# A one-core hybrid encoder layer: 896 columns of the expert table streamed and 1152 gathered, with a re-ordered ScalarE queue and filler matmuls

## What is computed

```python
scores = einsum('thcd,hcnd->thcn', q, keys)        # 8 heads, two halves of 128 keys
s_top, i_top = top_k(scores, 16)                   # 16 best of each half
best, pos = top_k(all 16*16 sums, 16)              # 16 experts for each head
idx = i*128 + j                                    # 128 experts for each token
gate = softmax(best)
hid = gelu(einsum('td,thkd->thk', x, U[idx]))      # U is 16384 x 2048
out = einsum('thk,thkd->td', gate * hid, V[idx])   # V is 16384 x 2048
```

## Time and profile before

| | us |
|---|---|
| median of 3 runs (2125.72 to 2132.07) | 2126.39 |
| the profiled execution: its own time | 2125.02 |
| its span, first to last instruction | 2123.0 |
| PE busy over the span | 2019.5 (95%) |
| DVE, ACT, POOL busy | 1508.4, 815.0, 835.2 |
| moved by DMA | 558.12 MB, mean 263 GB/s |
| mean granted TensorE clock | 0.911 |

### The profile page before, as it was taken

How to read it: one execution, slowest core, us unless ns; L and a number is a source line. 1 busy time by engine, 2 the same in 40 slices (tenths; PEclk the granted TensorE clock), 3 DMA queues, 4 the chain that set the end, 5 groups by cost and what they waited for, 6 DMA issues and landing times.

```text
span 2123.0 us, 27862 instructions
## 1 busy us (share of the span) xinstructions
PE 2019.5 (95%) x10247; PEld 1707.7 (80%) x10247; DVE 1508.4 (71%) x1987; ACT 815.0 (38%) x956; POOL 835.2 (39%) x626
## 2 busy tenths in 40 slices
PE   7999999999999999999999979997889999999997
PEld 6988998777888889988888757765556888888886
DVE  5465774556655557688888746666635999999998
ACT  4354433444434443222221223335436444444444
POOL 1001320000000001266654565566621888888782
PEclk9999999999999999999999965555559999999999
DMA  6555443445555565699999977677732999999996
GB/s 203 188 182 182 147 151 129 159 159 165 187 183 179 199 218 195 238 409 409 408 394 364 367 272 247 220 252 253 275 119 89 379 395 395 390 406 395 394 381 239
DMA packets 176353, 558.12 MB, mean 263 GB/s; under 512 B 19152, under 2 KB 22240, under 8 KB 175200
## 3 DMA queue, kind: packets, MB, share of 16 engines
q1 hardware_dynamic: 117744, 288.47, 38.6%
q0 software_dynamic: 58480, 267.94, 33.6%
HBM read 551.62 MB, written 4.72 MB: 262 GB/s over the span
## 4 chain that ended last, share of the span: by engine, by line
PE 77%; DMA 9%; DVE 6%; issue 3%; ACT 2%; POOL 2%; SPq 0%; DVEq 0%; POOLq 0%; ACTq 0%
PE acc L1918 7%; PE acc L1920 7%; PE acc L1919 7%; PE scr L2222 6%; PE acc L2180 5%; PE scr L2180 5%; PE acc L1901 4%; PE acc L1903 4%; PE acc L1904 4%; PE scr L2252 3%; DMA v_raw<-in_v_dense 3%; DMA ub<-in_u_dense 3%; PE acc L2306 3%; PE scr L2307 3%; PE acc L2307 3%
## 5 line engine op out<-in xcount | busy, mean ns | idle before, releaser
L1104 DVE TENSOR_TENSOR w_lo<-raw,w_hi 128x2048 fp32r<-128x2048 f32 x136 | 314.6, 2314 | 279.2 <-ACT w_hi L751 278.1
L751 ACT ACTIVATE w_hi<-raw 128x2048 fp32r<-128x2048 f32 x136 | 260.1, 1913 | 405.0 <-PE acc L1920 273.5
L707 POOL DMA_INDIRECT starts<-in_v_gather,expert x256 | 366.3, 1431 | 100.1 <-DVE X L1823 76.1
L684 POOL DMA_INDIRECT slots<-in_u_gather,expert x256 | 245.4, 959 | 269.2 <-DVE slots L1623 77.3
L1623 DVE SCALAR_TENSOR_TENSOR slots<-slots,acc 128x1280 f32<-128x1280 f32 x192 | 281.8, 1483 | 79.8 <-DMA slots<-in_u_gather,expert 78.2
L1042 ACT ACTIVATE v_hi<-v_raw 128x1344 fp32r<-128x1344 f32 x128 | 170.5, 1332 | 259.5 <-PE scr L2308 197.5
L1823 DVE SCALAR_TENSOR_TENSOR X<-starts,weight,X 128x704 f32<-128x704 f32 x256 | 242.1, 946 | 0.8 <-DMA starts<-in_v_gather,expert 0.4
L1918 PE MATMUL acc<-w_hi,hT_hi 128*128 128x512 f32 x576 | 227.6, 395 | 2.5 <-DVE w_lo L1104 2.5
L1919 PE MATMUL acc<-w_lo,hT_hi 128*128 128x512 f32 x576 | 225.3, 391 | 0.0
L1920 PE MATMUL acc<-w_hi,hT_lo 128*128 128x512 f32 x576 | 225.2, 391 | 0.0
L1840 DVE TENSOR_TENSOR v_lo<-v_raw,v_hi 128x1344 fp32r<-128x1344 f32 x128 | 199.3, 1557 | 8.8 <-issue 6.7
(11 more groups left out here) (322 smaller groups left out, 4003.6 us busy)
## 6 DMA issues: line engine op xcount, KB each, us to landing
raw<-in_w_in SPq DMA_DIRECT2D x88, 1024.0 KB, 5.1
v_raw<-in_v_dense SPq DMA_DIRECT2D x128, 672.0 KB, 7.5
ub<-in_u_dense SPq DMA_DIRECT2D x128, 384.0 KB, 7.2
raw<-in_w_o SPq DMA_DIRECT2D x16, 1024.0 KB, 5.1
raw<-in_peer_wq SPq DMA_DIRECT2D x16, 1024.0 KB, 5.3
raw<-in_w_a_up SPq DMA_DIRECT2D x8, 1024.0 KB, 5.0
raw<-in_w_b_up SPq DMA_DIRECT2D x8, 1024.0 KB, 5.1
slots<-in_u_gather,expert POOLq DMA_INDIRECT x256, 7.0
```

The source lines that it names most:

```text
L684: pool.indirect_dma_start(slots[j][:, :], None, u_gather[:, :], bass.IndirectOffsetOnAxis(ap=expert[:, t, k:k + 1], axis=0)).then_inc(row_ ...
L707: pool.indirect_dma_start(starts[j][:, :], None, v_gather[:, :], bass.IndirectOffsetOnAxis(ap=expert[:, s // NSEL, s % NSEL:s % NSEL + 1], ...
L751: a.activation(w_hi[:, m % 2, :, :], raw[:, m % 2, :, :], ACT.Copy).then_inc(hi_ready, 1)
L1104: v.tensor_tensor(w_lo[:, m % 2, :, :], raw[:, m % 2, :, :], w_hi[:, m % 2, :, :].bitcast(fp32), ALU.subtract).then_inc(lo_ready, 1)
```

## The change

Of U's 2048 columns seven blocks (896) are streamed and 1152 gathered. Streaming is spread over 162 gathers (40 groups) instead of 128 (32 groups), with three stream buffers of 3.5 KB for each partition instead of four of 3 KB. There are 21 row buffers of 4.5 KB instead of 20 of 5 KB; from gather 176 up to nine of them are open at a time, before it seven from gather 146 on (before: five to eight from gather 124 on, seven from 144). POOL multiplies a second row in every other group up to q = 112. In ScalarE's turn the evictions come first (`pairs`), and it sums the products of the group before; of a group's `hot_j` two stand ahead of that sum. The 64 picks are spread over 13 groups (41 to 53), the 32 first scatters over ten (54 to 63). Each pick has a filler matmul of 256 columns ahead of it; each first scatter has three of 512; and 16 of 512 stand behind the last dense block, ahead of the wait for the last eviction. The reads of kept rows have two buffers of the wider kind instead of three. The two halves of the residual have a semaphore each, the value gathers start five ahead instead of four, and the second streamed block of V is loaded with the first.

```diff
-UC = 6
+UC = 7
-UB_AT = (112, 120, 101, 104)
+UB_AT = (112, 120, 101)
+STREAMED = 162
+FOUR_GROUPS = STREAMED // FOUR
-CEN_GROUP = (13, 28)
-SELECT_FROM, SELECT_END = 34, 50
-MERGE_AT = 43
-GATE_TURN = 47
+CEN_GROUP = (15, 31)
+SELECTED_BY = 31
+SELECT_FROM, SELECT_END = 41, 54
+MERGE_AT = 48
+GATE_TURN = 51
-WARM_PICK, WARM_FIRST, WARM_LAST = 0, 0, 0
+WARM_PICK, WARM_FIRST, WARM_LAST, WARM_WAIT = 2 * P, 4 * P, 0, 16
+TWICE = 112
 def on_pool(q):
-    return q % FOUR == FOUR - 1 and FOUR <= q < GATHERS - 1 and q not in DVE_ALONE
+    return FOUR <= q < GATHERS - 1 and (q % FOUR == FOUR - 1 or q % (2 * FOUR) == 1 and q < TWICE)
+def pairs(i):
+    return [u for u in range(BLOCKS // 2) if 8 * u * FOUR_GROUPS // (4 * BLOCKS) == i]
 def parts(i):
-    return range(min(56, 2 * i), min(56, 2 * i + 2))
+    return range(min(56, 56 * i // SELECTED_BY), min(56, 56 * (i + 1) // SELECTED_BY))
...
                 for q in range(FOUR * n, FOUR * n + FOUR):
                     gather(q)
-                if on_pool(FOUR * n - 1):
-                    product(FOUR * n - 1)
+                for q in range(max(0, FOUR * n - FOUR), FOUR * n):
+                    if on_pool(q):
+                        product(q)
...
             for i in range(GROUPS):
+                for u in pairs(i):
+                    evict(u)
...
-                if 0 < i <= GROUPS // 2:
-                    evict(2 * i - 2)
-                    evict(2 * i - 1)
-                for b in selected(i):
+                sums = [q for q in range(max(0, FOUR * i - FOUR), FOUR * i) if on_pool(q)]
+                for b in selected(i)[0:2]:
+                    hot_j(b)
+                for q in sums:
+                    sum_product(q)
+                for b in selected(i)[2:]:
                     hot_j(b)
                 if i == SPREAD_FROM:
                     hot_first(0)
                 for n in spread(i):
                     hot_first(n + 1)
                     scatter_out(n)
-                if on_pool(FOUR * i + FOUR - 1):
-                    sum_product(FOUR * i + FOUR - 1)
...
+            pe.wait_ge(scr_free[1], use_number("score3"))
+            for n in range(WARM_WAIT):
+                warm(picked[0], GW)
             pe.wait_ge(evicted, BLOCKS // 2)
-            pe.wait_ge(scr_free[1], use_number("score3"))
             squares_j(0)
```

More of the change, by code:

```diff
@@ L135, in overwritten @@
         return None
-    return (P - 1 - (2 * block_at(j) + 9)) // 2
+    return int(P - 1 - (2 * (block_at(j) + ROW_KB) - 1)) // 2
 def row_open(j, q):
     if j < HELD_ROW:
-        return q < 2 * overwritten(j) - 4 and (q >= FOUR or j in FIRST_ROWS)
+        return q < 2 * overwritten(j) * STREAMED // P - 4 and (q >= FOUR or j in FIRST_ROWS)
     if j == HELD_ROW:
-        return FOUR <= q < P
-    return q >= (60 if j in SCORE_ROWS else 112 if j in ALL_ROWS else 144)
+        return FOUR <= q < 188
+    return q >= (64 if j in SCORE_ROWS else 128 if j in ALL_ROWS else 144 if j == NORM_ROW else 176)
 def row_table():
@@ L179, in selected @@
         return range(0)
-    per = NT * BATCHES // (SELECT_END - SELECT_FROM)
-    return range(per * (i - SELECT_FROM), per * (i - SELECT_FROM + 1))
+    n = SELECT_END - SELECT_FROM
+    return range(NT * BATCHES * (i - SELECT_FROM) // n, NT * BATCHES * (i - SELECT_FROM + 1) // n)
+def pairs(i):
+    return [u for u in range(BLOCKS // 2) if 8 * u * FOUR_GROUPS // (4 * BLOCKS) == i]
 def spread(i):
@@ L564, in _ @@
                 load_u(m)
[L565 to L568, removed]
+                for t in range(NT):
+                    if m == (FOUR * CEN_GROUP[t] + 6) * P // STREAMED:
+                        keep_rows(t)
             sp.wait_ge(cen_stored, 16 * NT)
+            sp.wait_ge(ones_ready, 1)
+            sp.sem_inc(granted_w, 1)
             for h in range(CHUNKS):
-                if h < 2:
-                    sp.wait_ge(ones_ready, h + 1)
-                    sp.sem_inc(granted_w, 1)
                 load_rows(h)
@@ L681, in gather @@
                     pool.wait_ge(u_used, BLOCKS)
-                    wait_rows(pool, HELD_ROW)
+                if first_use(q) and j == NORM_ROW:
+                    pool.wait_ge(product_ready, sum(map(on_pool, range(NSEL))))
                 pool.sem_inc(granted, 1)
@@ L1688, in centre, with ones @@
                                 ).then_inc(cen_ready, 1)
-            def ones(first):
+            def ones():
                 dve.wait_ge(cen_stored, 16 * NT)
-                if not first:
-                    dve.wait_ge(u_used, BLOCKS)
-                for room in (rows_a[0], rows_a[1], rows_b[0]) if first else (rows_a[2], rows_b[1], rows_b[2]):
+                for room in (*rows_a, *rows_b):
                     last = v.memset(room[:, :], 1.0)
@@ L1772, in _ @@
                             later_part(n)
-                    for b in selected(i)[q % FOUR:q % FOUR + 1]:
+                    n, at0 = len(selected(i)), q % FOUR
+                    for b in selected(i)[n * at0 // FOUR:n * (at0 + 1) // FOUR]:
                         find(b)
@@ L1782, in _ @@
                 if i == CEN_GROUP[1] + 3:
-                    ones(True)
-                if i == SELECT_FROM - 1:
-                    ones(False)
+                    ones()
                 if i in GATE_AT:
@@ L1795, in _ @@
                     copy_gate(0)
+                if i == SPREAD_FROM:
+                    wait_rows(dve, HELD_ROW)
                 for n in spread(i):
@@ L1806, in _ @@
             scatter_out(NT * BATCHES - 1)
-            dve.wait_ge(x_back, 16 * NT)
+            for t in range(NT):
+                dve.wait_ge(x_back[t], 16)
             def low_e(pair, t):
```

53 lines of the change are left out of this document (26 added, 27 removed).

## The result

The changed kernel takes 2322.0 us against 2128.7 before: the ratio is 1.091, with a 95% interval of 1.0885 to 1.0937. Slower was forecast, at 2200 us with a range up to 2235; the loss is 193 us where 75 were forecast. The profiled execution has a span of 2319.7 us.

What follows compares the result with a forecast made beforehand. Bounds: TensorE with DMA close by in the dense part, TensorE at half clock in picks, VectorE in values. Second scatters move from 1568 to 1643, +75 on 2125: 2200 us; case range 2180 to 2230, 8 in 10 from 2050 to 2235.

Steps and rivals of the forecast that it cites:

- Dense part, +55 for longer blocks: Dense part: fourteen TensorE instructions a block instead of twelve move its last matmul from 1230.4 to 1286 us, +55.
- the 17.6 us of waits: Dense part: TensorE's waits in the kernel before, 349.4 − 331.8, kept unchanged on top of 387 us of blocks.
- Three stream buffers: I take nothing: Dense part: three buffers need loads landing within about 5.6 us; nothing added to the sum, +46 us left to the range.
- a rival with a chance of 0.08: Dense part: the three-buffer ring binds, +46 us on the sum, 2246 us in all; chance 0.08.
- The argument that a shorter queue would bring the landing from 7.2 to 5.4 us: Dense part: a load has up to two others queued ahead instead of three, so the 7.2 us median becomes some 5.4.
- `keep_rows`, priced with other things at 0 to 10 us: Blocks 52 and 102, SP's queue: late rows stall the ring at most 10 us; with ScalarE's evictions, 0 to +10 together.
- The gap and the clock: Between dense part and picks: first pick after 11 us, some 7 us of TensorE idle, picks at clock 0.50.
- 2.75 + 0.21 = 2.96: Picks at clock 0.50: the 256-column filler adds 0.21 us to each, 64 picks take 194 us in all, ending at 1491.
- 3.15 + 3 × 0.43 = 4.44: First scatters at clock 0.50: three fillers of 0.43 us each; 32 take 142 us, 148 with waits of ten groups.
- The rival of a clock that stays up: Picks and first scatters: fillers close the gap, picks cost at most 1.85 us, kernel 2066 us (2040 to 2100); chance 0.34.
- Its deciding point: Gap before the picks: the clock stays up if TensorE idles under about 2 us between last filler and first pick.
- The rival of a clock that rises in the first scatters: First scatters: fillers and deep matmuls together raise the clock, 102 us for 148, kernel 2142 us (2115 to 2175); chance 0.16.

## Why the prediction was right in its direction and wrong in its size

- **Dense part, +55 for longer blocks: right in the price of a block, and with luck in the sum.** With four buffers it ends at 1289.0, 3 us from the 1286 forecast. But the 17.6 us of waits that the sum carries over from the kernel before are not those that were measured: with four buffers two waits behind `keep_rows` make 17.7 of the 17.9 us that TensorE waited for loads.
- **"Three stream buffers: I take nothing": wrong.** This is the first step that failed. The threshold was named (landing within 5.6 us; the median is 5.9 now) and the price nearly so (46 us; 40 and 52 measured), but as a rival with a chance of 0.08. No load landed within the 2.7 us worked out there for a load beside one gather; the least was 3.1 us before and 3.2 after. The argument that a shorter queue would bring the landing from 7.2 to 5.4 us went by the median. The median came out only 0.3 us above the threshold, and yet TensorE waited 36 times: loads that come late are paid one by one, and those that come early give nothing back. A sign of it was there. The prediction says, from the one row, that the chain of the dense part runs through TensorE alone and that TensorE ends every wait; but the chain of before also goes through eight stream loads of 8 to 10 us each, 19% of the stretch, the first of them here:

```profile
883.88 8.49 DMA ub<-in_u_dense
```

- **`keep_rows`, priced with other things at 0 to 10 us:** the wait behind it was 10.7 us in the changed kernel and 17.7 with four buffers, at the end of the bound or beyond it, and it was left out of the sum.
- **The gap and the clock: right.** First pick 10.5 us behind the dense part (forecast 11), 6.12 us of idle (forecast 7), 0.50 through picks and first scatters.
- **"2.75 + 0.21 = 2.96" for a pick: wrong.** This is the second step that failed, and the largest: 3.97 measured, 64 × 1.01 = 65 us. The filler was costed by its columns alone. That the row of 1270.83 has a twin, the second shallow matmul with the same start, stood in the trace of before; the earlier trace rows left it out, and with it the question of what a matmul on all 128 rows between the two does.
- **"3.15 + 3 × 0.43 = 4.44" for a first scatter: too small.** They are 5.02 us apart with fillers and 3.22 without: three fillers cost 1.80 us, not 1.29. The reason is not that of the picks, or not shown to be: the two shallow matmuls of a scatter lie on the same rows and start 0.6 us apart without fillers, so that no pair is parted. What the other 0.5 us are was not looked for.
- **What the three came to.** Of the 120 us that the second scatters start later than the 1643 forecast, 43 are the dense part, 64 the picks and 13 the first scatters.
- **The range.** Its upper end took each unknown cost alone. Ring and filler came together, and a range that adds 46 us to the 75 and leaves the filler without bounds can't reach 193.
- **The rival of a clock that stays up** was priced at 1.85 us a pick. With the strided operand the deep matmuls alone take 2.0 at either clock, so that this price was never there to be had. Its deciding point failed as well: with the gap covered to 0.69 us, less than its 2, the clock fell in the second pick, before and after the change. The rival of a clock that rises in the first scatters didn't come about either: 0.50 throughout, with TensorE busy for 163 of 165 us.

## What to carry to other kernels

Before an instruction is put between two others, read in the trace whether they overlap: its price is its own length and, at the least, the overlap that it ends. A ring of buffers is judged by how many loads land late, not by the median beside a threshold, and costs that are unknown and independent are added at the upper end of a range. Before fillers for the clock are paid for, one run shows whether they hold it in the stage itself: here two kernels with the gap covered but for 0.69 us took 2126.8 and 2324.3 us, as without the cover. And the way an operand lies in memory decides what the full clock is worth: eight deep matmuls took 2.00 us or 1.16.

## What the runs showed of the hardware

- A float32 matmul of 128 columns whose streamed entries lie 512 bytes apart took 0.25 us at 2.4 GHz and 0.26 at 1.2; side by side it took 0.14 at 2.4 GHz and 0.26 at 1.2.
- At 1.2 GHz matmuls on 5 and on 17 rows, in different groups of rows, started in the same moment, and the next work started 0.72 us later; with a matmul on 128 rows and 256 columns between them that was 0.72 + 0.52 + 0.72. Ahead of both, the same matmul made a pick only 0.2 us longer than without it.
- TensorE modelled busy for 253.3 of 257.6 us, fillers included, stayed at 1.2 GHz throughout; behind the residual's six deep matmuls (4.41 us without a break) the shallow ones took 0.50 us again, as before.
